# Bias products of a mixture-of-experts layer: two 64-row products in the halves of TensorE instead of two 128-row products

## The reference

```python
def expert_block(args):
    xb, e = args
    h = xb @ w_in[e] + b_in[e]
    glu = jnp.minimum(h[:, ::2], SWIGLU_LIMIT)
    lin = jnp.clip(h[:, 1::2], -SWIGLU_LIMIT, SWIGLU_LIMIT)
    act = glu * jax.nn.sigmoid(SWIGLU_ALPHA * glu) * (lin + 1.0)
    return act @ w_out[e] + b_out[e]
```

## Time and profile before

| what | value |
|---|---|
| median of three runs | 1555.06 us (1549.92 to 1555.36) |
| the profiled execution | 1550.04 us |
| its span | 1548.2 us |
| TensorE busy with matmuls | 1472.1 us, 95% |
| VectorE / ScalarE / GpSimd busy | 84% / 66% / 14% |
| granted TensorE clock, mean | 0.963 |

### The profile page before, as it was taken

The page is one execution under the profiler, slowest core; times in us unless marked ns, Lnnn a source line. Parts: engine busy times, 40 slices in busy tenths (PEclk is TensorE's granted clock), DMA queues, the critical chain, the costliest instruction groups (busy, mean ns, idle before and its releaser), DMA issues.

```text
span 1548.2 us, 23148 instructions
## 1 busy us (share of the span) xinstructions
PE 1472.1 (95%) x7337; PEld 1226.1 (79%) x7337; DVE 1293.1 (84%) x1136; ACT 1021.5 (66%) x910; POOL 212.8 (14%) x224
## 2 busy tenths in 40 slices
PE   7999789869999999999999999999999999999993
PEld 7999567738888888888888888888888888888882
DVE  5643662568999999999999999999999999999998
ACT  5222652226777777777777777777777777777773
POOL 0000202131111111111111111111111111111011
PEclk9999888859999999999999999999999999999997
DMA  9320001268999999999999999999999999999996
GB/s 282 114 88 28 1 1 55 65 179 310 359 359 376 362 374 363 372 369 379 373 366 363 371 371 366 371 361 381 368 374 371 362 368 365 375 369 373 354 374 258
DMA packets 139012, 467.08 MB, mean 302 GB/s; under 512 B 15629, under 2 KB 28209, under 8 KB 138920
## 3 DMA queue, kind: packets, MB, share of 16 engines
q1 hardware_dynamic: 125024, 445.17, 78.7%
q0 software_dynamic: 13200, 19.36, 3.8%
q10 hardware_dynamic: 760, 2.17, 0.4%
HBM read 463.50 MB, written 21.79 MB: 313 GB/s over the span
## 4 chain that ended last, share of the span: by engine, by line
PE 91%; DVE 3%; ACT 2%; DMA 2%; issue 1%; POOL 1%; POOLq 0%; SPq 0%; DVEq 0%; ACTq 0%
PE pair L880 23%; PE pair L882 23%; PE pair L888 23%; PE pair L619 3%; PE pair L624 3%; PE pair L620 3%; PE pair L856 2%; PE pair L895 2%; PE pair L906 2%; PE pair L769 1%; PE pair L770 1%; PE pair L777 1%; PE pair L676 1%; PE pair L799 1%; PE pair L653 0%
## 5 line engine op out<-in xcount | busy, mean ns | idle before, releaser
L1588 DVE TENSOR_TENSOR split<-ring,split 128x2048 fp32r<-128x2048 f32 x396 | 893.1, 2288 | 74.3 <-ACT split L1148 74.3
L1148 ACT CAST split<-ring 128x2048 fp32r<-128x2048 f32 x396 | 758.6, 1916 | 203.7 <-PE pair L888 193.3
L880 PE MATMUL pair<-split,operands 128*128 128x512 f32 x1584 | 631.0, 398 | 1.7 <-DVE operands L1609 1.7
L882 PE MATMUL pair<-split,operands 128*128 128x512 f32 x1584 | 618.7, 391 | 0.0
L888 PE MATMUL pair<-split,operands 128*128 128x512 f32 x1584 | 424.4, 390 | 0.0
L888 PEld LDWEIGHTS pair<-split,operands 128*128 128x128 f32 x1584 | 297.4, 188 | 63.2
L880 PEld LDWEIGHTS pair<-split,operands 128*128 128x128 f32 x1584 | 298.2, 188 | 61.4 <-issue 2.1
L882 PEld LDWEIGHTS pair<-split,operands 128*128 128x128 f32 x1584 | 298.4, 188 | 58.6
L1810 POOL DMA_INDIRECT expert_rows<-work,list_cur x33 | 44.6, 1352 | 503.5 <-PE pair L888 497.6
L1803 POOL DMA_INDIRECT work<-h_rows,token_next x35 | 80.0, 2285 | 198.0 <-DMA token_next<-slot_lists 174.4
L619 PE MATMUL pair<-split,operands 128*128 128x256 f32 x352 | 86.5, 283 | 1.0 <-DVE work L1321 1.0
(11 more groups left out here) (237 smaller groups left out, 1231.4 us busy)
## 6 DMA issues: line engine op xcount, KB each, us to landing
ring<-in_w_moe_in SPq DMA_DIRECT2D x264, 1024.0 KB, 8.0
ring<-in_w_moe_out SPq DMA_DIRECT2D x132, 1024.0 KB, 8.5
ring<-in_w_in SPq DMA_DIRECT2D x12, 1024.0 KB, 9.8
ring<-expert_rows SPq DMA_DIRECT2D x3, 2048.0 KB, 8.9
ring<-in_w_o SPq DMA_DIRECT2D x4, 1024.0 KB, 5.0
resid<-in_x SPq DMA_DIRECT2D x4, 512.0 KB, 5.6
h_rows<-work ACTq DMA_DIRECT2D x4, 512.0 KB, 2.8
late_ring<-expert_rows SPq DMA_DIRECT2D x4, 512.0 KB, 5.3
```

Of the source, the lines that this page charges most:

```text
L880: pe.matmul(dst[:, f, :], left_hi[:, k0 + k, :], hi[c.buffer][:, k, cols], start=(start and k == 0), stop=False)
L882: pe.matmul(dst[:, f, :], left_lo[:, k0 + k, :], hi[c.buffer][:, k, cols], start=False, stop=False)
L1148: act.copy(hi[c.buffer], raw[c.slot]).then_inc(hi_made, 1)
L1588: dve.tensor_tensor(lo[c.buffer], raw[c.slot], hi[c.buffer].bitcast(F32), ALU.subtract).then_inc(lo_made, 1)
```

## The change

The bias table is folded: instead of 64 rows by 2048 columns it has 128 rows by 1024 columns. Rows 0 to 63 hold the columns for f = 0 of both halves, rows 64 to 127 those for f = 1; in each group of 64, the first 32 rows are hi and the other 32 lo. The two products of `bias_of_half` then use 64 rows each, the first in rows 0 to 63, the second in rows 64 to 127, with separate banks as before. The one-hot operand fills 128 rows (four copies of the identity), and nothing is left to be zeroed. The table is loaded by four DMAs of 128 KB rather than two of 256 KB, from the same queue (32 rows of two pieces of 512 values each), and the lo part is made in two instructions.

```diff
-        b_in_rows = slot(RAW + 5).rearrange("p k c -> p (k c)")[0:2 * NE, :]
+        b_in_rows = slot(RAW + 5).rearrange("p k c -> p (k c)")[:, 0:FF]
-        expert_rows = w(21128, NE, 2 * NE)
+        expert_rows = w(21128, NE)
-        b_in_parts = operands[:, 4096:4096 + 2 * FF]
+        b_in_parts = operands[:, 4096:4096 + FF]
+        def b_in_of(f):
+            return b_moe_in[0].rearrange("e (g f c) -> f e g c", g=2, f=2)[f]
...
-            pe.wait_ge(b_in_split, 3)
+            pe.wait_ge(b_in_split, 2)
...
             def bias_of_half(g):
                 for f in range(2):
-                    at_f = (2 * g + f) * 512
-                    pe.matmul(pair[g][:, f, :], pick_bias, b_in_parts[:, at_f:at_f + 512], start=True, stop=False)
+                    rows = slice(2 * NE * f, 2 * NE * (f + 1))
+                    pe.matmul(pair[g][:, f, :], pick_bias[rows, :], b_in_parts[rows, g * 512:(g + 1) * 512],
+                              start=True, stop=False)
...
-            act.copy(b_in_parts[0:2 * NE, :], b_in_rows).then_inc(b_in_rounded, 1)
+            act.copy(b_in_parts, b_in_rows).then_inc(b_in_rounded, 1)
...
-            for still in (b_in_parts[2 * NE:P, :], pick_bias[2 * NE:P, :]):
-                dve.memset(still.bitcast(F32), 0.0).then_inc(b_in_split, 1)
             add_bias(2)
             add_bias(3)
-            low = slice(NE, 2 * NE)
-            dve.tensor_tensor(b_in_parts[low, :], b_in_rows[low, :], b_in_parts[low, :].bitcast(F32), ALU.subtract)\
-                .then_inc(b_in_split, 1)
+            for low in (slice(NE, 2 * NE), slice(3 * NE, 4 * NE)):
+                dve.tensor_tensor(b_in_parts[low, :], b_in_rows[low, :], b_in_parts[low, :].bitcast(F32), ALU.subtract)\
+                    .then_inc(b_in_split, 1)
...
-            for n in range(2):
-                pool.dma_start(b_in_rows[n * NE:(n + 1) * NE, :], b_moe_in[0]).then_inc(late_loaded[2], 16)
+            for n in range(4):
+                pool.dma_start(b_in_rows[n * NE:(n + 1) * NE, :].rearrange("e (g c) -> e g c", g=2), b_in_of(n // 2))\
+                    .then_inc(late_loaded[2], 16)
...
-            for n in range(2):
+            for n in range(4):
                 wait(pool, experts_listed, n)
                 pool.tensor_copy(expert_rows[n * NE:(n + 1) * NE, :],
                                  cst[n * NE:(n + 1) * NE, C_IDENT + n * NE:C_IDENT + (n + 1) * NE]).then_inc(experts_listed, 1)
-            pool.wait_ge(experts_listed, 2)
-            pool.wait_ge(late_loaded[2], 32)
+            pool.wait_ge(experts_listed, 4)
+            pool.wait_ge(late_loaded[2], 64)
...
-                pool.tensor_copy(pick_bias[0:2 * NE, :], expert_rows[:, e:e + 1].to_broadcast([2 * NE, SLOTS])
+                pool.tensor_copy(pick_bias, expert_rows[:, e:e + 1].to_broadcast([P, SLOTS])
```

More of the change, by code:

```diff
@@ L1645, in _ @@
             x_lo(0, 1)
-            dve.wait_ge(b_in_split, 3)
+            dve.wait_ge(b_in_split, 2)
             make_lo(0, 2)
@@ L1781, in pick @@
                     pool.sem_inc(pool_passed, 1)
-                pool.tensor_copy(pick_bias[0:2 * NE, :], expert_rows[:, e:e + 1].to_broadcast([2 * NE, SLOTS])
-                                 if isinstance(e, int) else expert_rows[:, bass.ds(e, 1)].to_broadcast([2 * NE, SLOTS]))\
+                pool.tensor_copy(pick_bias, expert_rows[:, e:e + 1].to_broadcast([P, SLOTS])
+                                 if isinstance(e, int) else expert_rows[:, bass.ds(e, 1)].to_broadcast([P, SLOTS]))\
                     .then_inc(pick_ready, 1)
```

## The result

The changed kernel's median is 1567.65 us (1561.93 to 1573.76, eight runs) against 1554.15 us (1549.92 to 1557.31, eight runs) for the kernel before, a ratio of 1.0086 with a 95% interval of 1.0056 to 1.0116. The forecast was 1566.7 us, +0.75%. The ratios of this document leave out two far slower executions, one of twelve with late issue (2649.25 us) and one of twelve with one trip and late issue (5105.32 us).

What follows compares the result with a forecast made beforehand. TensorE was taken to bound the expert passes. Row changes less the shared stream gave +10.6 us over 66 halves, extra DMA issues +1.0, so +11.6 on the median of 1555.06: 1566.7 us, range 1559 to 1572, low end extended to 1556.

Steps and rivals of the forecast that it cites:

- What bounds the kernel: Expert passes: TensorE's stream sets the pace, so a nanosecond added or taken there goes into the time as it is.
- What is removed: Bias products of a half: two run side by side in one stream of 0.213 us instead of 0.45, removing 0.24 us.
- What is added: Around each bias pair: two changes of row layout, 128 to 64 rows and back, at 0.197 us each.
- The sum for a half: Each half of a pass: 0.607 us and about 0.01 against 0.453, so +0.16 us, times 66 = +10.6 us.
- Before the passes: GpSimd's DMA issues ahead of the last iota: four instead of two for the bias table, +1.03 us.
- What was costed at nothing: Before the passes: identity copies, table landing, L1752, ScalarE, VectorE and 128-row pick changes, covered by idle time, worth nothing.
- The median: Whole run: 1566.7 us, +0.75% against the median of 1555.06, given 70%.
- The range: Whole run: 1559 to 1572 us, its low end extended to 1556 for part of the cases with no change.
- Signs named ahead: Trace of a pass: pair 0.42 us long, starting 0.31 behind L888, starts within 0.02, passes longer by 0.32 us.
- A free or half-hidden change: Borders of the bias pair: row change free, 1541.2 us (8%), or half hidden, about 0.1 us each, 1553.5 us (12%).
- Products that don't run side by side: Bias pair: no sharing, so +0.394 us a half, 1582.1 us in all; chance 7%.
- TensorE as no bound: Passes: the DMA share of 0.99 would hide the 0.16 us a half, leaving 1556.1 us; chance 3%.

Runs made afterwards that it cites:

- late issue: The kernel before with the load issues of both bias tables moved behind the iotas VectorE waits for: 1546.9 us, ratio 0.9977 to the kernel before.
- one trip and late issue: Changed kernel, second half's and next pass's first half's bias products issued together, bias-table loads issued behind the iotas: 1547.16 us, ratio 0.9965 to the kernel before.
- four loads: The kernel before with its bias table loaded by four DMAs of half the columns each: ratio 1.0018 to the kernel before.
- tables alone: The changed kernel's folded table and four loads, but each bias product over all 128 rows with a half-zero one-hot operand: ratio 1.0024 to the kernel before.
- both on the same rows: The kernel before with both bias products of a half on rows 0 to 63: ratio 1.0185 to the kernel before.

## Why the prediction was right

**What bounds the kernel: right.** TensorE's matmuls wait no more in the passes after the change than before it, and taking the bias out took its 0.91 us a pass in full.

**What is removed: right, a little too high.** The products share the array, 3 ns apart. I took off 0.24 us a half (0.45 less a stream of 0.213). By the starts one of two spacings of 227 ns goes, less 3.

**What is added: right.** I had 0.197 us a change from the retention's narrow float32 products. On these fp32r products it is 0.199 on the way in (91 + 108) and 0.205 on the way back (95 + 110), 0.404 a half, where I had 0.394. The Trainium skill, "TensorEngine Tiling (Array Packing)", Key Properties, says that a change of tiling mode drains TensorE. The traces agree: 91 to 95 ns of a change are TensorE running empty, as read from the starts, and the exposed load is the rest.

**The sum for a half: +0.16 us forecast, +0.20 measured.** 0.404 - 0.224 = 0.180 stands at the pair itself (1087 - 907 ns). A further 0.02 stands in the five products behind it, spaced up to 236 ns before they fall back to 227, as they also do behind the transposes. I had no term for that. From the start of the first pair to that of the last it is 1161.9 us against 1149.5, so the passes lost 12.4 us, where I had 10.6 for all 66 halves; this is inside the bounds I gave (9.2 to 12.9).

**Before the passes: the term right, its effect left open.** +1.03 us forecast for the two issues, +1.12 measured up to the add. Whether all of it reaches the end is less sure. In the changed kernel's profiled execution the chain then runs into the store of the normalized rows:

```profile
304.34 1.30 DVE work L1492
305.65 19.96 DMA h_rows<-work
```

In four loads the store began 4.8 us later and took 3.7 us less:

```profile
310.44 16.23 DMA h_rows<-work
```

So it may take up part of what is gained or lost ahead of it; how much, no run shows. Four loads alone show 0.95 us at the add and nothing at the same clock, but tables alone with the same four issues is 0.9 us slower and late issue 1.3 us faster. What was costed at nothing cost nothing visible, except that the pick of 128 rows takes 0.40 rather than 0.36 us, which nobody waits for.

**The median: met in part by luck.** At the same clock the change costs 14.3 us, where my sum is 11.6. The eight executions of the changed kernel lie in two groups, four at 1561.93 to 1562.86 us (clock 0.965 to 0.967) and four at 1572.44 to 1573.76 us (0.957 to 0.958), so the median of 1567.65 is a middle in which no execution lies. That the forecast of 1566.7 meets it within 1 us is luck; that the time falls into the range is not. The range itself was added up loosely: +7.6 to +16.8 on 1555.06 with 2 us either side is 1560.7 to 1573.9, not 1559 to 1572.

**Signs named ahead:** the pair 0.42 us (0.43), 0.31 us behind L888 (0.318), 0.32 us from the first product behind it to the next (0.338 by the starts; the chain, which goes by ends, gives that product 0.43), starts within 0.02 us (0.003), passes longer by 0.32 us (0.41).

**The rivals.** A free or half-hidden change is out: the loads behind a change show 0.24 to 0.35 us of idle time before them. Products that don't run side by side are the kernel with both on the same rows, +1.85%, a pass of 36.33 us and 335 ns between the two starts; the change shows 35.89 us and 3 ns. TensorE as no bound is out by the kernel without bias.

## What to carry to other kernels

Packing two half-height products side by side saves one stream, but a trip to 64 rows and back costs 0.40 us, nearly two products of 512 columns. It pays only if more than two streams are saved on one trip, so collect such products and issue them together; with one pair per trip it loses 0.18 us at the pair (0.20 with the spacings behind it), with two pairs it breaks even. These prices hold for fp32r products of 512 columns at the full clock; no run here has more than two pairs on a trip. Before such a change, look in the trace for a place where products of different heights already alternate, and read the price of the change there.

## What the runs showed that I had not expected

The load is exposed in the second place as well: behind a change of rows the first product's load and the empty array add up, and the spacing stays up to 9 ns wider for five products after the return (0.02 us a half). With the bias gone, the DMA engines delivered 378 GB/s at a share of 1.00, though in the same stretch the share had been 1.00 at 368 GB/s too: the share of busy time doesn't tell how much room is left. Moving DMA issues of GpSimd behind the iotas went with a higher TensorE clock from 248 to 298 us (1.00 and 0.93 rather than 0.83 to 0.86). And an issue on GpSimd's queue took 0.50 to 0.55 us for 128 KB and for 256 KB alike.
